# A two-block transformer layer on one core: weight splitting moved ahead in the second block, GpSimd held back, halves streamed around a wait

## The reference

```python
# first block
q_lat, kv_lat, k_rope, dq, dk, dv, gate_pre = split(rmsnorm(x) @ w_in)
q  = rmsnorm(q_lat) @ w_uq;  kv = rmsnorm(kv_lat) @ w_ukv      # 8 heads, 64 plain + 32 rotary
o_mla  = causal_attention(q, k, v)                             # first attention
o_diff = rmsnorm(attn(dq0, dk0, dv) - lam * attn(dq1, dk1, dv))  # second attention, 4 heads
x = x + (g_mla * (o_mla @ wbm) + g_diff * (o_diff @ wbd)) @ w_out
x = x + (silu(h @ w_gate) * (h @ w_up)) @ w_down               # h = rmsnorm(x)
# second block
h = rmsnorm(rmsnorm(x));  q, k, v, za, u, vs, zs, gm = split(h @ w_in_2)
q, k = partial_rope(q), partial_rope(k)                        # 16 query heads, 2 key heads
a = (window_attention(q, k, v) * silu(za)) @ w_att_out
y = ga * a + gs * (spatial_gating(u, vs, zs) @ w_sg_out);  out = rmsnorm(x + y @ w_o)
```

## Time and profile before

| | |
|---|---|
| median of 3 runs | 1313.05 us |
| the profiled execution's own time | 1313.46 us |
| its span in the trace | 1311.7 us |
| mean granted clock of TensorE | 0.992 |
| DVE busy | 702.0 us, 54% |
| ACT busy | 527.8 us, 40% |
| POOL busy | 55.5 us, 4% |

### The profile page before, as it was taken

One profiled execution on the slowest core, in us unless ns is written; L12 is line 12 of the kernel. 1 busy time (PEld: TensorE's weight loads), 2 busy tenths in 40 slices (PEclk: granted clock), 3 DMA queues, 4 the chain that ended last, 5 costly groups with the idle time before them and its releaser, 6 DMA issues.

```text
span 1311.7 us, 15823 instructions
## 1 busy us (share of the span) xinstructions
PE 1277.9 (97%) x6212; PEld 1065.5 (81%) x6212; DVE 702.0 (54%) x1073; ACT 527.8 (40%) x889; POOL 55.5 (4%) x97
## 2 busy tenths in 40 slices
PE   8999999999999999999999998999999999999997
PEld 6877778877888888888888886888988888888885
DVE  6875566644555444444443358756554536436554
ACT  5545555652334343434322333336553334223222
POOL 0001331211000000000000000000000000000000
PEclk9999999999999999999999998999999999999998
DMA  5232323122432332333223323331104233332321
GB/s 194 69 96 65 80 74 89 50 65 67 171 116 78 115 96 96 96 96 112 96 80 104 104 72 100 102 97 33 35 31 144 97 96 96 96 96 97 95 82 64
DMA packets 106362, 119.53 MB, mean 91 GB/s; under 512 B 13814, under 2 KB 88636, under 8 KB 106300
## 3 DMA queue, kind: packets, MB, share of 16 engines
q1 hardware_dynamic: 106160, 118.64, 29.0%
q10 hardware_dynamic: 140, 0.04, 0.0%
HBM read 113.42 MB, written 2.10 MB: 88 GB/s over the span
## 4 chain that ended last, share of the span: by engine, by line
PE 92%; DVE 5%; ACT 2%; issue 1%; POOL 1%; DVEq 0%; ACTq 0%; POOLq 0%
PE ps_mm L1925 58%; PE ps_mm L1960 21%; PE ps_o L2332 2%; PE ps_o L2112 1%; PE ps_s L2089 1%; DVE w_lo L1150 1%; PE ps_t L2312 1%; PE ps_mm L1931 1%; PE ps_mm L2020 1%; PE ps_t L2099 1%; PE ps_s L2133 1%; PE ps_o L2155 1%; PE ps_s L2297 1%; PE ps_s L2295 1%; ACT w_hi L638 1%
## 5 line engine op out<-in xcount | busy, mean ns | idle before, releaser
L1925 PE MATMUL ps_mm<-act_hi,w_hi 128*128 128x512 f32 x944 | 374.2, 396 | 8.4 <-DVE w_lo L1150 6.9
L1925 PE MATMUL ps_mm<-act_lo,w_hi 128*128 128x512 f32 x944 | 371.7, 394 | 0.0
L1925 PE MATMUL ps_mm<-act_hi,w_lo 128*128 128x512 f32 x944 | 371.5, 393 | 0.0
L1150 DVE TENSOR_TENSOR w_lo<-stage,w_hi 128x2048 fp32r<-128x2048 f32 (+3 forms) x77 | 157.5, 2045 | 167.2 <-ACT w_hi L638 167.1
L1925 PEld LDWEIGHTS ps_mm<-act_hi,w_hi 128*128 128x128 f32 x944 | 178.4, 189 | 45.5 <-DVE w_lo L1150 8.9
L1925 PEld LDWEIGHTS ps_mm<-act_hi,w_lo 128*128 128x128 f32 x944 | 178.3, 189 | 35.8
L1925 PEld LDWEIGHTS ps_mm<-act_lo,w_hi 128*128 128x128 f32 x944 | 178.4, 189 | 34.7
L638 ACT ACTIVATE w_hi<-stage 128x2048 fp32r<-128x2048 f32 (+3 forms) x78 | 133.0, 1706 | 165.4 <-PE ps_mm L1960 118.9
L1561 DVE TENSOR_TENSOR w_lo<-stage,w_hi 128x2048 fp32r<-128x2048 f32 x23 | 52.7, 2292 | 56.3 <-ACT w_hi L920 56.2
L1960 PE MATMUL ps_mm<-w_hi,h_hi 128*128 128x512 f32 x176 | 68.8, 391 | 0.0
L1960 PE MATMUL ps_mm<-w_hi,act_hi 128*128 128x512 f32 x176 | 68.6, 390 | 0.0
(11 more groups left out here) (388 smaller groups left out, 1979.3 us busy)
## 6 DMA issues: line engine op xcount, KB each, us to landing
stage<-in_w_in SPq DMA_DIRECT2D x44, 1024.0 KB, 5.4
stage<-in_w_ffn_gate SPq DMA_DIRECT2D x11, 1024.0 KB, 5.3
stage<-in_w_ffn_up SPq DMA_DIRECT2D x11, 1024.0 KB, 5.3
stage<-in_w_ffn_down SPq DMA_DIRECT2D x10, 1024.0 KB, 5.0
stage<-in_w_out SPq DMA_DIRECT2D x4, 1024.0 KB, 5.1
stage<-in_w_att_out SPq DMA_DIRECT2D x4, 1024.0 KB, 5.3
stage<-in_w_sg_out SPq DMA_DIRECT2D x4, 1024.0 KB, 5.3
stage<-in_w_o SPq DMA_DIRECT2D x4, 1024.0 KB, 5.0
```

The costliest lines, as they stand in the source:

```text
L1150: V.tensor_tensor(w_lo[:, s, 0:k * w], stage[:, s, 0:k * w], w_hi[:, s, 0:k * w].bitcast(F32), ALU.subtract).then_inc(w_lo_made, 1)
L1925: ins = T.matmul(ps_mm[:, 2 * bank_slot + m, :], wt[:, kk, m * P:(m + 1) * P], acts[ap][:, kk, :], start=(r == 0), stop=(r == per - 1), sk ...
```

## The change

Four places are touched; no amount of arithmetic changes.

- POOL waits for `lat_scaled` to reach 8 before its two multiplications of the rotary tables.
- The rotary query parts of the first attention go to `dq`, not to `prob`; the last four `spread_q` move from steps 0 and 1 to steps 4, 6, 8 and 10; the waits of steps 2 and 3 for them go. DVE makes the two halves of the keys' weights behind value copies 1 and 2 (counted from 0), before the loop; value copy 3 comes in step 0.
- In steps 10, 14 and 18 of the second attention, half of the streamed matmuls stand ahead of the wait for `od_made`.
- In the second block ACT makes `hi(q2+2)` before its loop, and then `hi(q2+i+2)` at the head of turn i. DVE makes `lo(q2+2)` before it waits for the turned norms, and `lo(u + 2)` at the head of turn i; the `lo(za)` of the keys' bank goes, since turn 3 has it. PE turns the norms after 12 of the 48 matmuls of q2+1.

```diff
+    def pieces(self, p, part=(0, 1)):
+        a, n = self.cuts[p], self.cuts[p + 1] - self.cuts[p]
+        a, b = (a + int(n * x) for x in part)
...
             pool.wait_ge(xr_spread, 1)
+            pool.wait_ge(lat_scaled, 2 * TT)
...
-                nc.scalar.activation(qm[MN:MQ, h, :], prob[32 * (h % 4):32 * (h % 4) + 32, 2 + h // 4, :],
+                nc.scalar.activation(qm[MN:MQ, h, :], dq[32 * (h % 4):32 * (h % 4) + 32, h // 4, :],
...
-                    if p in (2, 3):
-                        act.wait_ge(q_spread, 4 * (p - 1))
...
-                if p < 2:
-                    spread_q(4 + 2 * p)
-                    spread_q(5 + 2 * p)
+                if p in (4, 6, 8, 10):
+                    spread_q(2 + p // 2)
...
             down_squares(1, 3)
+            hi(uq2 + 2)
             for i in range(4):
+                if i:
+                    hi(uq2 + i + 2)
                 for m in range(2):
-                    if m:
-                        hi(uq2 + i + 2)
...
-            for t in range(TT):
+            def keep_values(t):
                 V.tensor_copy(vm[:, t, :], bank(U0["mv"], t)).then_inc(bank_free, 1)
+            keep_values(0)
+            keep_values(1)
+            lo_half(U0["dk"], 0)
+            keep_values(2)
+            lo_half(U0["dk"], 1)
...
-                if p < 2:
-                    lo_half(U0["dk"], p)
+                if p == 0:
+                    keep_values(3)
...
             rsqrt_of(8, made=3)
+            lo(U0["q2"] + 2)
...
                 if i:
-                    lo(u + 1)
+                    lo(u + 2)
...
             u = U0["kv2"]
-            lo(u + 1)
             rope_bank(u, 0, kv[:, 1, :], rope2, swap8, 1.0, k_roped, 1)
...
+                turned = 7 <= q < NP and (q - 7) % 4 == 0
+                if turned:
+                    stream(DIFF_STREAM, p, streamed, (0, 0.5))
...
-                    if q >= 7 and (q - 7) % 4 == 0:
+                    if turned:
                         pe.wait_ge(od_made, (q - 7) // 4 + 1)
...
+                stream(DIFF_STREAM, p, streamed, (0.5, 1) if turned else (0, 1))
...
-            straight(uq2 + 1, "F", acts_x, 0, 24)
+            straight(uq2 + 1, "F", acts_x, 0, 12)
             pe.wait_ge(rstd_made, 3)
...
-            straight(uq2 + 1, "F", acts_x, 24, 48)
+            straight(uq2 + 1, "F", acts_x, 12, 48)
```

More of the change, by code:

```diff
@@ L140, in started @@
         return self.starts.get(p, ())
-    def pieces(self, p):
-        a, b = self.cuts[p], self.cuts[p + 1]
+    def pieces(self, p, part=(0, 1)):
+        a, n = self.cuts[p], self.cuts[p + 1] - self.cuts[p]
+        a, b = (a + int(n * x) for x in part)
         return [(self.first + i, max(a, n0) - n0, min(b, n0 + n) - n0)
@@ L1378, in _ @@
                     if u == U0["qp"]:
-                        rope_bank(u, m, prob[:, 2 + m, :], rope_m, swap16, MQ ** -0.5, qp_roped, m + 1)
+                        rope_bank(u, m, dq[:, m, :], rope_m, swap16, MQ ** -0.5, qp_roped, m + 1)
                         if m == 0:
@@ L1976, in straight, with stream @@
                      chunk_waits=chunk_waits, w_by_chunk=w_by_chunk)
-            def stream(st, p, acts):
-                for u, a, b in st.pieces(p):
+            def stream(st, p, acts, part=(0, 1)):
+                for u, a, b in st.pieces(p, part):
                     straight(u, "F", acts(u), a, b)
@@ L2137, in _ @@
                 q = p - LAG
+                turned = 7 <= q < NP and (q - 7) % 4 == 0
+                streamed = lambda u: om if u < U0["gate_b"] and (u - U0["gate_m"]) % 2 else acts_x
+                if turned:
+                    stream(DIFF_STREAM, p, streamed, (0, 0.5))
                 if 0 <= q < NP:
@@ L2147, in _ @@
                     ins.then_inc(diff_t_full, 1)
-                stream(DIFF_STREAM, p, lambda u: om if u < U0["gate_b"] and (u - U0["gate_m"]) % 2 else acts_x)
+                stream(DIFF_STREAM, p, streamed, (0.5, 1) if turned else (0, 1))
                 if 0 <= q < NP:
```

## The result

| | before | after |
|---|---|---|
| median, us | 1313.01 (4 runs, 1312.66 to 1313.55) | 1301.59 (4 runs, 1301.54 to 1302.51) |
| the profiled execution | 1313.46 | 1302.51 |
| its span | 1311.7 | 1300.8 |
| mean granted clock | 0.992 | 0.996 |

The ratio is 0.9915, 95% interval 0.9903 to 0.9926: the kernel is 11.4 us faster. The forecast was 1302.4.

The account below looks back on a forecast made before the run. PE, busy 1277.9 of 1311.7 us, was taken to set the time; gains 2.4 + 3.0 + 3.2 + 2.0 = 10.6 off 1313.46 gave 1302.9, less 0.4, 1302.4 us; the forecast's own range was 1300.0 to 1305.0.

Parts of the forecast that it names:

- Part 1: GpSimd's multiplications held back at the latents: PE's first product behind the transposes comes earlier, gain 2.4 us.
- (b): First query unit: POOL's moved multiplications beat DVE's lo, the latents' gain becomes -0.5 us, total 1305.3 us; chance 0.12.
- Part 2: First attention, keys' weights between value copies: 1.3 us of idleness and 1.7 of slow clock saved, gain 3.0 us.
- Part 3: Second attention, half the streamed matmuls ahead of three waits: stalls covered, gain 3.2 us, bounds 2.4 and 3.3.
- Part 4: Second block, query weights earlier: 8.8 us gained at q2+2, less a new stall, its clock and handovers, net 2.0 us.
- the stall at za+1: Second block: PE stands 4.2 us for lo(za+1), with 2.4 us more lost to the slow clock behind it.
- (a): Second block: no new stall at za+1, so the gain there is 8.8 us, total 1295.6 us; chance 0.13.
- (c): First attention: four late spread_q on ACT delay PE and its clock falls, 1315 to 1322 us; chance 0.03.
- (d): All four places: waits only move, PE meets each a few instructions later, 1312 to 1314 us; chance 0.02.

Follow-up runs that it names:

- E8: Kernel after, with GpSimd's two multiplications held back further, until the latents' lo is made: 1301.42 us, ratio to before 0.9916.
- E1: Kernel before, with only GpSimd's two multiplications made to wait for the scaled latents: 1310.38 us, ratio 0.9981.
- E12: E1's kernel executed and profiled once more, with no edit: 1310.77 us, ratio 0.9982.
- E3: Kernel before, with only half of the streamed matmuls moved ahead of the three waits on od: 1308.85 us, ratio 0.9966.
- E4: Kernel before, with only the second block's query weights made one unit ahead of the rotary work: 1311.37 us, ratio 0.9987.
- E10: Kernel before, with only the spreads of heads 4 to 7 late and from dq, DVE's order as before: 1312.80 us, ratio 1.0002.
- E9: Kernel after, with the spreads of heads 4 to 7 again in steps 0 and 1 of the first attention: 1302.88 us, ratio 0.9927.
- E7: Kernel after, with 16 matmuls of unused result put into PE's stall ahead of za+1: 1300.48 us, ratio to before 0.9907.
- E5: Kernel after, with ACT's hi again between the two banks' copies of a turn, for the unit one further ahead: 1295.46 us, ratio to before 0.9873.
- E6: Kernel after, with hi(za+1) on ACT ahead of the wait for the keys' rotation and its copies: 1299.77 us, ratio to before 0.9897.

## Why the prediction was right

**Part 1** (2.4, measured 2.34). The two short instructions went to 0.17 us, the wait of 1.99 us and the half clock under the transposes went with them, and the first product starts 4.30 us behind the cut, where I had 60.3 - 56.06 = 4.24. The 0.3 us that I charged for `lo` running into GpSimd is 0.2, shown by E8. The form of it looks different: by its row `lo` was not held back until GpSimd's first multiplication had ended, but started at 57.82, right when ACT's `hi` was done (56.95 + 0.84), and took 1.16 us instead of 0.96. The Trainium skill, "SBUF — State Buffer", section "SBUF: two separate sides", has the loser blocked for the whole instruction. By half the pair of the earlier trace rows, 1.41 us, GpSimd's first would end at 58.30 and `lo` at 59.26; it ended at 58.98, and free of GpSimd it would have at 58.78. The trace shows a delay, but a smaller one than that working gives. If `lo` did wait for the whole of GpSimd's first, this one ended at 58.02, 1.13 us behind its start in the profile; GpSimd's rows are too rough to tell that from ports that are shared. Rival (b), which needed `lo` to lose to both, is out.

**Part 2** (3.0, measured 3.25). Third scores 0.15 us later for their exponential (I had 0.25), no wait behind them, clock up. The idleness and the clock were sized rightly, but the clock's share was not part 2's alone: E1 and E12 keep all of the idleness and have no slow clock, 1.65 us less than before. Either part spares that term, and a sum of parts measured one by one would count it twice. Why the clock stays up in E1 and not in before, E3, E4 and E10 is not shown; E1 and E12 are the two without the stall and slow clock at the latents, but E3 had the clock up there too and fell here, so that is no sufficient reason. The times and mean clocks of E1's and E12's other executions suggest that the same kernel can go either way. The late `spread_q` cost nothing (137.60 in both), as forecast; that their move was needed is shown for 0.5 us only (E9).

**Part 3** (3.2, measured 3.64, above my upper bound of 3.3). The bound was too tight by the way that I read it. The idle column sums to 3.25, but a row of PE lasts longer than it holds up the next instruction, so that the first part of each stall stands as busy. In E3, where nothing waits there, the instruction behind the rows that stood ahead of the three stalls starts 0.06, 0.06 and 0.36 us after them; in before it was 1.01, 1.02 and 2.25. From start to start the stalls were 3.80 us long, 0.55 more than the column says. Of these 3.64 were gained; where the other 0.16 went is not shown. No new wait for the next exponential is in the list, where I had feared up to 0.2 us.

**Part 4** (2.0, measured 2.08). Each link of the chain of reasons held: 1.86 us of DVE's idleness per turn (I had 1.8), the stall at za+1 4.07 us (4.2), the slow clock behind it 2.1 us by E7 and, with E5, 6.81 - 4.07 - 0.38 = 2.36 (2.4). E5 shows that the order of ACT's queue is the cause, and rival (a), no new stall, is what E5 makes true: 1295.46 us where that rival said 1295.6. The agreement of the sum owes something to the execution it was made against: from q2 to the end, the six profiles with the old order take 522.25 to 523.63, on average 522.87, and before's is the longest. Four with the new order (E4, after, E8, E9) average 521.22, so that part 4 is worth 1.65 us on average, as E4's 1.7 says.

**The other rivals.** (c), the late spreads slowing the first attention, is refuted by the unchanged stretch behind it. (d), that the waits only move, is true of one of the four places, at a price that stood in the sum.

## What to carry to other kernels

When a wait is removed by making an operand one unit earlier, follow the queue of each engine that makes it up to the last unit: here the move put ACT's half of the work behind copies that it used to run between, and 6.8 of 8.9 us came back as a stall four units later. Move such a step ahead in units and keep its place among its neighbours (E5). Price a stall as idleness plus clock, take the clock term as a range of a microsecond or more even for the same stall, and compare traces by stretches between the same instructions, where 0.1 us can be told as long as the clock stays up, although the medians tell 1.3.

## What the runs showed of the chip

- The same idle time of PE was followed by different clocks: behind 0.64 and 1.53 us at the third scores 0.72, 1.00 or 0.50 over the next 6 us, and behind 1.99 us at the latents half clock in before (part 1's stretch 6.64 us) and full clock in E3 (5.65 us; window of PE below). The two profiled executions of one kernel, E1 and E12, agreed; the others of that kernel, and the one of E6 at 1297.35 us, look as if the outcome differs between executions. What decides was not found. The Trainium skill, "TensorE: Matmul & The Clock Gate", section "What's actually happening", says that the monitor of the clock runs freely and is not reset when a kernel starts, so that the same code can meet it at another point; the scatter agrees with that, and no run here shows it.

```profile
58.50:66.00 7.50, 5.34 (x34) 1.00 0.33 52
```

- Once down, the clock cost 3.0 us behind a stall of 5.81 us in before and 1.6 in E3 (46.64 and 45.24 against 192 x 0.2275 = 43.7 us), because in E3 it fell earlier in the stall: the slow time that lies over idleness costs nothing.
- A stall of 1.54 us behind a short one of 0.38 (E6) was followed by half clock, one of 1.66 us in the second attention before was not the earlier trace rows.
- Sixteen matmuls in a stall of 4 us kept the clock at 1.00 behind it, and won 2.1 us without anything being ready earlier (E7).
- GpSimd's pair took 3.23 us beside DVE's `lo`, 2.83 beside the short instructions and 2.99 in E8, and `lo` 1.16 us beside it and 0.96 alone.
